# Two rows of layer 1's modulation move from the ctx attention to the heads of two feed forwards

## The chip, the cores and the metric

The kernel runs on one core of one Trainium2 chip. The metric is the device time of one execution in microseconds (us), the median of the runs.

## The reference

The program computes two blocks on 256 tokens of width 1024, all in float32. The first block has two layers; each is a feed forward, a mixer (convolution, recurrence, pool), a cross attention and a second feed forward, with a layer norm behind each. The second block also has two layers, on the output of the first and on a ctx stream of 256 tokens; each has an attention and a PEER feed forward, and both are modulated by six vectors per layer:

```python
def swiglu(x, w_gate, w_up, w_down):
    return (jax.nn.silu(x @ w_gate) * (x @ w_up)) @ w_down
...
for l in range(DEPTH):                       # first block
    h = layer_norm(ALPHA * h + 0.5 * swiglu(h, ffn1...), ...)
    ...mixer, layer_norm; cross_attn, layer_norm...
    h = layer_norm(ALPHA * h + 0.5 * swiglu(h, ffn2...), ...)
...
mod = silu(c) @ ada_w[i] + ada_b[i]          # second block, layer i: 6 x 1024 values, for c and for c_ctx
```

The modulation of layer 1 is what the change moves about: a product of two vectors of 1024 values (for the two conditions) with a 1024 x 6144 matrix.

## The kernel before, in words

**Two streams of work.** TensorE (PE) is led through one long sequence. First comes the ctx stream of the second block's layer 0: modulation, QKV, an attention over the ctx (functions `ctx_attention`), the output projection and the PEER scores. Then comes the first block with its four feed forwards, two per layer. Beside the feed forwards VectorE (DVE) does the PEER work of the ctx stream: GpSimd (POOL) gathers expert rows of 1024 values by indirect DMAs, and DVE dots and sums them. Last comes the second block.

**Weights in chunks.** Most weights pass through a ring `wring` of four slots, each a chunk of 128 x 1024 float32 (512 KB). SyncE (SP) issues the loads in a fixed order (`load`, `chunk_loads`, L495 to L510); each waits until the chunk before in its slot is released (`chunk_done`). Feed forward weights have places of their own in `ring` (`ff_loads`, L512 to L518), three parts per tile and two tiles deep, but their loads stand in the same queue of SP. What SP waits for holds back all that stands behind it in the order.

**Rows of the modulation.** Layer 1's modulation has 6144 columns, made in 12 rows of 512 columns. A row takes four chunks, one turn of the ring (`mod_row_loads`, L528). It is multiplied in one of two ways. PE does it alone (`mod_row_part`, L833 to L843): eight matmuls of 128x2 by 128x512, two records each in the trace. Or DVE does it (`mod_row_sums`, L3084 to L3098): eight instructions scale the row's parts by the condition and add them up in `row_acc`, and PE sums that over the partitions with one product (L1526, two records). The last of the eight instructions releases all four chunks at once. Either way ScalarE (ACT) copies the 2x512 result and stores it (`mod_row_take`, L1749 to L1766).

**Where the rows stood.** Rows 0 and 1 are multiplied by PE in the ctx attention (L1146 to L1161), row 2 in the PEER scores of the ctx (L1265). In each layer of the first block, one row is summed by DVE at the end of each of the two feed forwards, and one is multiplied by PE in the layer norm behind the cross attention and one in the norm behind the second feed forward. The last row comes at the second block's start.

**The ctx attention.** It has four units of heads. For each, PE computes scores (L1124), DVE takes the maximum and negates it (L2578, L2580), ACT takes the exponentials (four pieces), DVE divides by the sum (L2587, L2589), PE transposes the probabilities (L1133), ACT copies them, and PE multiplies them with the values (L1142). PE's order is written out by hand: scores 0, half of row 0, scores 1, the other half, transposes and values of unit 0, scores 2, row 1, unit 1, scores 3, unit 2, unit 3, then the output projection (L763). DVE puts tiles of the first layer's modulation (`ada_tiles`, L2362 to L2376, two instructions of 128x1024 each that matter here) between its softmax steps; the gated add of the projection is L2598.

**A feed forward.** It has 22 tiles: the first, five turns of a loop of four, and the last. For each tile PE makes gate and up (L1494, 32 records), ACT applies silu, DVE multiplies (`hidden_tile`, L3064), and PE adds the down product (L1502, 16 records) one tile later. DVE's sum of a row stands behind the loop, ahead of the last hidden tile; its column sum on PE stands between the last two down products. The row's chunks are loaded ahead of the loop, so that they lie ready. The loads of the next chunks (the norm's row, or the first mixer weights) stand behind the loop's in SP's queue and wait for the release by DVE's sum.

## Time and profile before

| | |
|---|---|
| median of 3 runs | 3305.03 us (3302.08 to 3306.79) |
| profiled execution, its own time | 3290.4 us |
| its span | 3288.5 us |
| PE busy | 3084.1 us (94%) |
| PE weight loads (PEld) | 2185.8 us (66%) |
| DVE busy | 2111.8 us (64%) |
| POOL busy | 1221.7 us (37%) |
| ACT busy | 951.1 us (29%) |
| DMA | 1165.52 MB, mean 354 GB/s |

The profiled execution is one run, and its time can be set against its span only; the median comes from other runs. Busy shares are means over stages with different limits. In a row of the timeline the first number is the start in us from the span's begin, the second the duration; "x8" stands for eight instructions drawn together, and the bracket tells how long the engine was idle before it and what ended that.

### The profile page before, as it was taken

The numbers are of one execution on the slowest core, as the hardware profiler recorded it, in microseconds if no ns is written. First come the engines' busy times: TensorE is split into PE (matmuls) and PEld (weight loads), VectorE is DVE, ScalarE is ACT, GpSimd is POOL, SyncE is SP. The second block draws the span as 40 slices with busy tenths as digits, with TensorE's granted clock in tenths as the row PEclk, the third lists the DMA queues.
The fourth block names the chain that finished last, engine by engine and source line by source line (L and its number), as shares of the span: only waits on it lengthen the run. The fifth ranks groups of instructions, "written<-read, shape, count | busy, mean of one in ns | idle before, by whom it ended". The sixth has DMA issues, their size and how long they took to land.

```text
span 3288.5 us, 39667 instructions
## 1 busy us (share of the span) xinstructions
PE 3084.1 (94%) x13217; PEld 2185.8 (66%) x13217; DVE 2111.8 (64%) x4281; ACT 951.1 (29%) x2489; POOL 1221.7 (37%) x1129
## 2 busy tenths in 40 slices
PE   8999999999999999999999999978989999997777
PEld 5598888887887888887886755533435855542224
DVE  6776787766555456765455596577565587587544
ACT  2310012121001002221002364335446464444333
POOL 1003554343444442353440144434444045454332
PEclk9999999999999999999999999999999999999999
DMA  9687988788998996788996799999999799999998
GB/s 351 215 299 287 374 339 305 267 325 338 356 347 336 365 345 231 242 326 338 370 355 241 292 421 420 420 419 404 410 422 420 293 419 421 421 421 422 421 421 356
DMA packets 252614, 1165.52 MB, mean 354 GB/s; under 512 B 27321, under 2 KB 34969, under 8 KB 186417
## 3 DMA queue, kind: packets, MB, share of 16 engines
q0 software_dynamic: 152784, 825.30, 62.3%
q1 hardware_dynamic: 99632, 338.30, 28.4%
q8 instruction: 80, 1.31, 0.2%
q14 instruction: 70, 0.57, 0.0%
q10 hardware_dynamic: 48, 0.05, 0.0%
HBM read 1162.44 MB, written 1.10 MB: 354 GB/s over the span
## 4 chain that ended last, share of the span: by engine, by line
PE 65%; DMA 17%; DVE 7%; ACT 5%; issue 2%; SPq 0%; POOL 0%; ACTq 0%; DVEq 0%; POOLq 0%
PE ps_b L1494 18%; PE ps_a L1432 13%; DMA ring<-in_peer_uv,idx 12%; PE ps_a L1502 9%; PE ps_b L776 6%; PE ps_a L763 5%; ACT arena L1721 3%; DVE ring L2883 2%; DMA arena<-in_peer_uv,idx 2%; DMA wring<-in_second_w 2%; PE ps_b L785 1%; PE ps_b L1261 1%; ACT L1721 1%; PE ps_b L1202 1%; PE ps_b L1254 1%
## 5 line engine op out<-in xcount | busy, mean ns | idle before, releaser
L1432 PE MATMUL ps_a<-ring,arena 128*128 128x512 f32 x1728 | 823.3, 611 | 131.0 <-ACT arena L1721 130.4
L738 POOL DMA_INDIRECT ring<-in_peer_uv,idx x448 | 498.4, 1112 | 888.7 <-PE ps_a L1432 624.7
L2883 DVE SCALAR_TENSOR_TENSOR ring<-ring,h_tm 128x1024 f32<-128x1024 f32 x448 | 546.6, 1222 | 381.7 <-DMA ring<-in_peer_uv,idx 381.0
L697 POOL DMA_INDIRECT ring<-in_peer_uv,idx_now x512 | 577.1, 1127 | 427.9 <-DVE arena L2711 163.8
L1432 PEld LDWEIGHTS ps_a<-ring,arena 128*128 128x128 f32 x1728 | 309.3, 192 | 564.5 <-ACT arena L1721 291.3
L1494 PE MATMUL ps_b<-x_t,ring 128*128 128x256 f32 x2816 | 623.6, 380 | 2.0 <-DMA ring<-in_ffn 1.1
L1494 PEld LDWEIGHTS ps_b<-x_t,ring 128*128 128x128 f32 x2816 | 533.0, 190 | 81.5 <-issue 3.5
L1721 ACT ACTIVATE arena<-ps_b 128x256 f32<-128x256 f32 (+3 forms) x226 | 103.6, 460 | 1254.7 <-PE ps_b L1494 829.5
L1502 PE MATMUL ps_a<-arena,ring 128*128 128x256 f32 x1408 | 318.7, 380 | 0.0
L2711 DVE SCALAR_TENSOR_TENSOR arena<-ring,h_tm 128x1024 f32<-128x1024 f32 x256 | 299.4, 1219 | 25.0 <-DMA ring<-in_peer_uv,idx_now 24.5
L1502 PEld LDWEIGHTS ps_a<-arena,ring 128*128 128x128 f32 x1408 | 267.5, 190 | 39.3 <-issue 3.5
L1721 ACT ACTIVATE wts<-dots 128x1 f32<-128x1 f32 (+1 forms) x514 | 103.7, 202 | 606.3 <-DVE ring L2883 523.6
L3064 DVE SCALAR_TENSOR_TENSOR arena<-ps_b,arena 128x256 f32<-128x256 f32 x88 | 37.3, 424 | 336.3 <-PE ps_b L1494 193.1
L1721 ACT ACTIVATE arena<-consts,wts 128x128 f32<-128x128 f32 x512 | 205.5, 401 | 66.5 <-PE ps_a L1432 20.7
L776 PE MATMUL ps_b<-x_t,wring 128*128 128x256 f32 x896 | 197.8, 381 | 6.6 <-ACT x_t L1721 6.6
L2720 DVE SCALAR_TENSOR_TENSOR arena<-ring,stage,arena 128x1024 f32<-128x1024 f32 x160 | 195.1, 1277 | 4.0 <-DMA ring<-in_peer_uv,idx_now 3.9
L776 PEld LDWEIGHTS ps_b<-x_t,wring 128*128 128x128 f32 x896 | 166.9, 190 | 34.0 <-issue 8.1
L763 PE MATMUL ps_a<-arena,wring 128*128 128x256 f32 (+1 forms) x896 | 169.1, 350 | 1.9 <-DMA wring<-in_second_w 1.0
L763 PEld LDWEIGHTS ps_a<-arena,wring 128*128 128x128 f32 x896 | 150.6, 191 | 20.1 <-issue 2.0
L1721 ACT ACTIVATE wts<-wts,gates 128x1 f32<-128x1 f32 x512 | 150.7, 294 | 16.6
L2720 DVE SCALAR_TENSOR_TENSOR arena<-ring,wts,arena 128x1024 f32<-128x1024 f32 x92 | 115.0, 1287 | 49.5 <-DMA ring<-in_peer_uv,idx_now 49.5
L1721 ACT ACT_TABLE_LOAD x107 | 137.3, 1283 | 12.0 <-PE ps_b L1494 8.7
(444 smaller groups left out, 3341.0 us busy)
## 6 DMA issues: line engine op xcount, KB each, us to landing
ring<-in_ffn SPq DMA_DIRECT2D x264, 512.0 KB, 7.1
wring<-in_second_w SPq DMA_DIRECT2D x174, 512.0 KB, 5.3
wring<-in_mix_w SPq DMA_DIRECT2D x128, 512.0 KB, 5.7
ring<-in_ada_rows POOLq DMA_DIRECT2D x36, 512.0 KB, 6.3
ring<-in_second_w SPq DMA_DIRECT2D x12, 1024.0 KB, 9.9
ring<-in_peer_uv,idx_now POOLq DMA_INDIRECT x512, 8.6
ring<-in_peer_uv,idx POOLq DMA_INDIRECT x448, 14.8
arena<-in_second_w SPq DMA_DIRECT2D x13, 512.0 KB, 8.1
```

What stands on the lines that cost most here:

```text
L697: G.indirect_dma_start(rows[:, s, :], None, table, bass.IndirectOffsetOnAxis(ap=idx_now[:, half, s:s + 1], axis=0)).then_inc(rows_in[s], p ...
L738: G.indirect_dma_start(pairs[slot].rearrange("p c d -> p (c d)"), None, a["peer_uv"], bass.IndirectOffsetOnAxis(ap=idx[:, b, s:s + 1], axi ...
L763: ins = mm(acc_t[:, j, cols], w[:, k * P:(k + 1) * P], src[:, k, cols], start=k == 0, stop=k == KT - 1)
L776: ins = mm(bank[:, t * T:(t + 1) * T], w[:, k * P:(k + 1) * P], src[:, k, :], start=k == 0, stop=k == KT - 1)
L1432: ins = mm(ps_a[:, b * D + j * 512:b * D + (j + 1) * 512], diags[:, at % DIAGS, :], pairs[at % PAIRS][:, 1, j * 512:(j + 1) * 512], start= ...
L1494: ins = mm(bank[:, part * T:(part + 1) * T], fw[:, ft % 2, part, k * P:(k + 1) * P], x_t[:, k, :], start=k == 0, stop=k == KT - 1)
L1502: ins = mm(acc_t[:, j, :], fw[:, ft % 2, 2, j * P:(j + 1) * P], hidden[:, ft % 2, :], start=False, stop=last, skip_group_check=True)
L1721: return nc.scalar.activation(out, in_, func, **k)
L2711: V.scalar_tensor_tensor(acc[s % 2], rows[:, s, :], 1.0, h, ALU.mult, ALU.mult, accum_out=out).then_inc(row_used, ve.adds(row_used))
L2720: ins = V.scalar_tensor_tensor(acc[s % 2], rows[:, s, :], w, acc[s % 2], ALU.mult, ALU.add)
L2883: V.scalar_tensor_tensor(row, row, 1.0, h_tm[:, n // SLOTS, :], ALU.mult, ALU.mult, accum_out=dots[:, n % SLOTS:n % SLOTS + 1]).then_inc(d ...
L3064: V.scalar_tensor_tensor(hidden[:, ft % 2, :], ps_b[:, (ft % 2) * 512 + T:(ft % 2 + 1) * 512], 0.5, silu[:, ft % 2, :], ALU.mult, ALU.mult ...
```

## The change

- **ctx attention.** Rows 0 and 1 are no longer multiplied there; the only row of the ctx stage (row 0) is the one in the PEER scores. The output projection's weights (WO) are loaded right behind QKV's, ahead of row 0. DVE's order becomes: three times "weights of unit u, maximum of unit u+1, one modulation tile", then the weights of unit 3 and two tiles. Before, one tile stood behind unit 3.
- **Head of two feed forwards.** Row 3 is summed by DVE ahead of the first hidden tile of layer 0's second feed forward, row 6 at the same place of layer 1's first. Their chunks are loaded where the end's row was loaded before, ahead of the loop. PE's column sum for them (`row_total`) stands behind the loop, ahead of the last tile's gate and up; ACT takes it ahead of the last silu.
- **End of the same two.** Their end rows (4 and 7) remain, but their loads now stand behind the loop's loads in SP's queue. DVE's sum of any row but the first waits until PE has summed the row before (`row_summed`), as both use `row_acc`.
- The other rows keep their places with new numbers: `FF_ROWS` at the ends, `NORM_ROWS` in the norms, and `ROW_AT` maps row numbers to columns.

```diff
--- before
+++ after
@@ -54,8 +54,9 @@
 MOD_ROWS = ADA_CHUNKS // WR
-CTX_MOD_ROWS = 3
-ROW_AT = 0, 1, 2, 4, 3, 5, 6, 7, 8, 9, 10, 11
+CTX_MOD_ROWS = 1
+ROW_AT = 0, 4, 1, 5, 6, 2, 7, 8, 3, 9, 10, 11
+FF_ROWS, HEAD_ROWS, NORM_ROWS = ((1, 4), (7, 9)), (3, 6), ((2, 5), (8, 10))
@@ -71,6 +72,9 @@
 ROW_LOADS = (FIRST_ADA - WR + QKV_CHUNKS + WO_CHUNKS + 2 * PQ_CHUNKS) // WR + CTX_MOD_ROWS + 1
+MIX_LOADS = MIX_CHUNKS // WR
+ROW_TURNS = {row: ROW_LOADS + turns for row, turns in (
+    (1, 0), (3, MIX_LOADS + 2), (4, MIX_LOADS + 3), (6, MIX_LOADS + 5), (7, MIX_LOADS + 6), (9, 2 * MIX_LOADS + 8))}
@@ -532,10 +536,8 @@
             eng.dma_start(subk, a["subk"]).then_inc(subk_in, 16)
+            chunk_loads(a["second_w"], FIRST_ADA + QKV_CHUNKS, WO_CHUNKS)
             mod_row_loads(0)
-            mod_row_loads(1)
-            chunk_loads(a["second_w"], FIRST_ADA + QKV_CHUNKS, WO_CHUNKS)
-            mod_row_loads(2)
             chunk_loads(a["second_w"], FIRST_ADA + PQ_AT, PQ_CHUNKS)
@@ -546,25 +548,28 @@
             for l in range(L):
-                mix_at, row_at = l * MIX_CHUNKS, CTX_MOD_ROWS + 4 * l
+                mix_at = l * MIX_CHUNKS
                 for w in range(2):
...
                             ff_loads(l * (2 * FT) + (w * FT + ft), ft, part)
-                    if w == 0:
-                        mod_row_loads(row_at)
+                    if w == 1:
+                        chunk_loads(a["mix_w"], mix_at + (MIX_CHUNKS - WR), WR)
+                        mod_row_loads(NORM_ROWS[l][0])
+                    if w != l:
+                        mod_row_loads(HEAD_ROWS[l])
                     else:
-                        chunk_loads(a["mix_w"], mix_at + (MIX_CHUNKS - WR), WR)
-                        mod_row_loads(row_at + 1)
-                        mod_row_loads(row_at + 2)
+                        mod_row_loads(FF_ROWS[l][w])
                     with sp.loop(FT_TURNS, **ff_turn) as i:
...
                                 ff_loads(i * FT_STEP + (l * (2 * FT) + (w * FT + 2 + ft)), ft, part)
+                    if w != l:
+                        mod_row_loads(FF_ROWS[l][w])
                     if w == 0:
...
                     else:
-                        mod_row_loads(row_at + 3)
+                        mod_row_loads(NORM_ROWS[l][1])
             def place_load(place, chunk_at, landed):
@@ -1133,9 +1138,7 @@
                     ins.then_inc(pt_done, pe.adds(pt_done))
-                if u < 2:
-                    mod_row_free()
-                else:
+                if u >= 2:
                     eng.wait_ge(pv_taken, pe.next(pv_taken))
@@ -1147,12 +1150,9 @@
                 qk_stats(4, 3, False)
-                mod_row_part(0, 0, 2)
                 ctx_scores(1)
-                mod_row_part(0, 2, WR)
                 ctx_weighted(0)
                 ctx_scores(2)
-                mod_row_part(1, 0, WR)
                 ctx_weighted(1)
@@ -1481,7 +1481,17 @@
-            def feed_forward(h_ready):
+            def row_total():
+                pe.skip(chunk_done, WR)
+                for arrived in weights_in:
+                    pe.skip(arrived, 16)
+                eng.wait_ge(chunk_done, pe.now(chunk_done))
+                mod_row_free()
+                mm(ps_d[0:2, :], mean_d[:, 0:2], row_acc, start=True, stop=True).then_inc(
+                    row_summed, pe.adds(row_summed))
+                pe.skip(mod_row_taken, 1)
+
+            def feed_forward(h_ready, two_rows):
@@ -1517,15 +1527,11 @@
                         down(q)
+                if two_rows:
+                    row_total()
                 gate_up(FT - 1)
                 down(FT - 2)
-                pe.skip(chunk_done, WR)
-                for arrived in weights_in:
-                    pe.skip(arrived, 16)
-                eng.wait_ge(chunk_done, pe.now(chunk_done))
-                mm(ps_d[0:2, :], mean_d[:, 0:2], row_acc, start=True, stop=True).then_inc(
-                    row_summed, pe.adds(row_summed))
-                pe.skip(mod_row_taken, 1)
+                row_total()
                 down(FT - 1, True)
@@ -1582,7 +1588,7 @@
             for l in range(L):
-                feed_forward(h_take if l else h_have)
+                feed_forward(h_take if l else h_have, l == 1)
                 layer_norm(value_between)
@@ -1691,7 +1697,7 @@
                 layer_norm(mod_row_between, True)
-                feed_forward(h_take)
+                feed_forward(h_take, l == 0)
                 layer_norm(mod_row_between, l + 1 < L)
@@ -1942,12 +1948,10 @@
                 exps(0)
-                mod_row_take(0, 0, ada_row[0])
                 turned(0)
...
                 exps(2)
-                mod_row_take(1, 1, ada_row[1])
                 turned(1)
@@ -2006,7 +2010,7 @@
                 act(lbs[:, 8:16], lbs[:, 0:8], ACT.Exp).then_inc(lb_exp, ac.adds(lb_exp))
-                mod_row_take(2, 1, ada_row[0])
+                mod_row_take(0, 1, ada_row[0])
                 for b in range(NB):
@@ -2191,7 +2195,7 @@
-            def feed_forward():
+            def feed_forward(head_row=None):
                 def tile(ft):
@@ -2203,6 +2207,8 @@
                         ac.skip(hidden_done, 1)
+                if head_row is not None:
+                    mod_row_take(head_row, 2, mod_row)
                 eng.wait_ge(hidden_done, ac.now(hidden_done))
@@ -2223,10 +2229,9 @@
             for l in range(L):
-                row_at = CTX_MOD_ROWS + 4 * l
                 eng.wait_ge(layer_vecs, ac.next(layer_vecs))
-                feed_forward()
-                mod_row_take(row_at, 2, mod_row)
+                feed_forward(HEAD_ROWS[1] if l == 1 else None)
+                mod_row_take(FF_ROWS[l][0], 2, mod_row)
                 layer_norm(0)
@@ -2253,7 +2258,7 @@
                     if g == 8:
-                        eng.wait_ge(mod_row_out[row_at % 2], ac.now(mod_row_out[row_at % 2]))
+                        eng.wait_ge(mod_row_out[FF_ROWS[l][0] % 2], ac.now(mod_row_out[FF_ROWS[l][0] % 2]))
                     group(g, dst)
@@ -2309,11 +2314,11 @@
                 layer_norm(2)
-                mod_row_take(row_at + 1, 1, mod_row)
-                feed_forward()
-                mod_row_take(row_at + 2, 2, mod_row)
+                mod_row_take(NORM_ROWS[l][0], 1, mod_row)
+                feed_forward(HEAD_ROWS[0] if l == 0 else None)
+                mod_row_take(FF_ROWS[l][1], 2, mod_row)
                 layer_norm(3)
-                mod_row_take(row_at + 3, 1, mod_row)
+                mod_row_take(NORM_ROWS[l][1], 1, mod_row)
@@ -3026,16 +3031,12 @@
             qk_norm(3, False, 0)
-            ve.skip(chunk_done, 2 * WR)
-            ctx_over(0)
-            ctx_max(1)
-            ada_tiles(1)
-            ctx_over(1)
-            for u in range(2, 4):
-                ctx_max(u)
-                ada_tiles(4 - u)
+            for u in range(3):
                 ctx_over(u)
-            ada_tiles(1)
+                ctx_max(u + 1)
+                ada_tiles(1)
+            ctx_over(3)
+            ada_tiles(2)
             ve.skip(pt_done, 8)
@@ -3081,13 +3082,14 @@
-            def mod_row_sums(l, w):
-
-                loads = ROW_LOADS + l * (MIX_CHUNKS // WR + 4) + w * (MIX_CHUNKS // WR + 2)
+            def mod_row_sums(row):
+
+                if row > CTX_MOD_ROWS:
+                    eng.wait_ge(row_summed, ve.next(row_summed))
                 for k in range(KT):
...
                     if k % 2 == 0:
-                        eng.wait_ge(weights_in[k // 2], 16 * loads)
+                        eng.wait_ge(weights_in[k // 2], 16 * ROW_TURNS[row])
                     if k == 0:
@@ -3119,13 +3121,12 @@
                     if q == FT - 2:
-                        mod_row_sums(0, 0)
+                        mod_row_sums(FF_ROWS[0][0])
                 eng.wait_ge(row_used, ve.now(row_used))
...
                 eng.wait_ge(dve_step, ve.now(dve_step))
-                for i, out_done in enumerate(mod_row_out):
-                    eng.wait_ge(out_done, 16 * ((CTX_MOD_ROWS + 1 - i) // 2))
+                eng.wait_ge(mod_row_out[0], 16 * CTX_MOD_ROWS)
                 V.memset(attn, 0.0).then_inc(dve_step, ve.adds(dve_step))
@@ -3134,6 +3135,8 @@
+                if w != l:
+                    mod_row_sums(HEAD_ROWS[l])
                 hidden_tile(0)
@@ -3143,7 +3146,7 @@
                     turn_end(summing, i, at + HEAD_SLOTS)
-                mod_row_sums(l, w)
+                mod_row_sums(FF_ROWS[l][w])
                 hidden_tile(FT - 1)
```

## Rows read from the trace of the kernel before

**Rows 1.** The page's chain of work that ended last, share of the span by engine
```profile
PE 65%; DMA 17%; DVE 7%; ACT 5%; issue 2%; SPq 0%; POOL 0%; ACTq 0%; DVEq 0%; POOLq 0%
```

**Rows 2.** Busy us: PE, PEld, DVE, ACT, POOL; PE clock, DMA share, GB/s
```profile
86.00:127.00 41.00, 34.26 (x117) 15.19 (x116) 30.99 (x44) 18.60 (x50) 2.65 (x5) 1.00 0.52 175
...
775.00:975.00 200.00, 199.61 (x924) 175.25 (x923) 105.78 (x106) 7.51 (x20) 93.12 (x92) 1.00 0.97 365
```

**Rows 3.** Timeline, ctx attention: start, us, engine, line, operation, out<-in, idle before <-releaser
```profile
88.82 3.60 PE L839 MATMUL ps_b<-wring,cond 128*2 128x512 f32 x8
...
93.91 1.22 DVE L2589 TENSOR_TENSOR arena<-arena,stats 128x1024 f32<-128x1024 f32 x1
...
100.31 1.96 PE L1142 MATMUL ps_b<-arena,vals 128*128 128x512 f32 x4 [1.42 <-ACT arena L1721]
...
102.10 1.89 PE L1124 MATMUL ps_a<-keys_t,arena 128*128 128x256 f32 x8
...
103.92 7.03 PE L839 MATMUL ps_b<-wring,cond 128*2 128x512 f32 x16
...
105.49 0.47 ACT L1721 ACTIVATE arena<-ps_a,stats 128x256 f32<-128x256 f32 x1 [2.59 <-DVE stats L2580]
...
106.85 0.48 ACT L1721 ACTIVATE arena<-ps_a,stats 128x256 f32<-128x256 f32 x1
...
111.88 0.60 ACT L1721 ACTIVATE arena<-ps_c 128x512 f32<-128x512 f32 x1 [0.31 <-ACT arena L1721]
...
114.90 1.89 PE L1124 MATMUL ps_a<-keys_t,arena 128*128 128x256 f32 x8
...
122.25 0.66 PE L1133 MATMUL ps_c<-consts,arena 128*128 128x128 f32 x4 [1.80 <-DVE arena L2589]
...
124.17 1.95 PE L1142 MATMUL ps_b<-arena,vals 128*128 128x512 f32 x4 [0.83 <-ACT arena L1721]
...
126.86 27.87 PE L763 MATMUL ps_a<-arena,wring 128*128 128x256 f32 x128 [0.73 <-issue]
...
134.15 0.88 DVE L2598 SCALAR_TENSOR_TENSOR ctx_t<-ps_a,mods,ctx_t 128x256 f32<-128x256 f32 x2 [4.15 <-PE ps_a L763]
```

**Rows 4.** Timeline, two pauses of PE, and busy times just behind the second
```profile
39.02 9.32 PE L776 MATMUL ps_b<-arena,wring 128*128 128x256 f32 x32 [3.10 <-ACT arena L1721]
...
2940.50 2.99 PE L1432 MATMUL ps_a<-ring,arena 128*128 128x512 f32 x4 [2.90 <-ACT arena L1721]
...
2942.00:2943.00 1.00, 1.00 (x2) 0.34 (x1) 1.00 (x9) 0.73 (x3) 0.00 (x0) 0.50 1.04 434
```

**Rows 5.** Timeline, DVE's first hidden tile of layer 0's second feed forward
```profile
768.41 0.42 DVE L3064 SCALAR_TENSOR_TENSOR arena<-ps_b,arena 128x256 f32<-128x256 f32 x1 [6.99 <-PE ps_b L1494]
```

**Rows 6.** Timeline, end of layer 0's second feed forward
```profile
965.84 10.69 SPq L515 DMA_DIRECT2D ring<-in_ffn  x4
...
975.87 7.07 PE L1494 MATMUL ps_b<-x_t,ring 128*128 128x256 f32 x32
...
978.76 5.75 DVE L3095 SCALAR_TENSOR_TENSOR arena<-wring,cond,arena 128x512 f32<-128x512 f32 x7
...
984.53 2.16 SPq L498 DMA_DIRECT2D wring<-in_second_w  x4
...
986.32 1.02 PE L1526 MATMUL ps_d<-arena,consts 128*2 128x512 f32 x2
...
987.27 3.72 PE L1502 MATMUL ps_a<-arena,ring 128*128 128x256 f32 x16
...
990.92 1.45 PE L839 MATMUL ps_b<-wring,cond 128*2 128x512 f32 x3
```

**Rows 7.** DMA at that end: busy times, then issues from 984 and from 970 us
```profile
975.00:985.00 10.00, 10.00 (x48) 8.82 (x47) 9.48 (x13) 0.38 (x1) 3.91 (x4) 1.00 0.89 319
...
wring<-in_second_w SPq DMA_DIRECT2D x3, 512.0 KB, 5.6
...
ring<-in_ffn SPq DMA_DIRECT2D x7, 512.0 KB, 10.3
```

## The prediction

> **What bounds the kernel now.** I read the chain of waits first: TensorE (PE) holds 65% of it, DMA 17%, VectorE (DVE) 7% [rows 1]. Then the busy times by stretch, because a share over the whole span hides that the two places touched have different limits. In the loop of a feed forward PE is busy for 199.6 of 200 us while DVE has 94 us free and the DMA engines are at 0.97 [rows 2]. In the ctx attention PE is busy for 34 of 41 us and the DMA engines are at 0.52 [rows 2]. Last I read the timeline of the ctx attention [rows 3]: 14 us of PE's time there is the product of two modulation rows. It stands between the steps of a softmax, in which PE, ScalarE (ACT) and DVE wait for each other in turn. So one must ask which of these PE microseconds anybody waits for. A PE microsecond in a feed forward, by contrast, is paid in full.
>
> **Sum, part 1: two rows leave the ctx attention.** Removed are 32 matmul records on PE (3.60, as much again later, and 7.03 us [rows 3]), two ACT copies, two stores and 4 MB of loads (eight chunks of 0.52). I rebuild the chain with the intervals of the trace that stay:
> - The weights of unit 0 are ready at 95.13 (93.91 + 1.22). The transposes now start there. From transposes to the value product it is 1.92 us (122.25 to 124.17), from there to the scores of unit 2 1.79 us (100.31 to 102.10), from these to unit 2's exponentials 3.39 us (102.10 to 105.49). That gives 102.3 instead of 105.49.
> - The exponentials take 1.84 us (105.49 to 106.85 + 0.48). ACT's own order puts the copies of unit 1's transposes behind them, so these come at 104.2 instead of 111.88; the 7.03 us of PE's row work had pushed them far beyond. From those copies to unit 3's scores it is 3.02 us (111.88 to 114.90), so 107.2 instead of 114.90.
> - From there to the output projection at 126.86 nothing changes. **The term is -7.7 us** [rows 3]. The other 6.5 us of removed PE work become pauses.
>
> DVE must not take PE's place. One tile of the first layer's modulation moves behind the last softmax step, ahead of the first gated add. DVE idles 4.15 us before that add [rows 3], a tile costs two instructions of 1.22 us as the other 128x1024 ones here: hidden. The loads of the output weights now directly follow QKV in SyncE's (SP's) queue: earlier, never later.
>
> **Part 2: the clock in the new pauses.** Without the row work two PE pauses of about 3.5 us appear: one where 3.6 us of it stood ahead of unit 0's transposes, one ahead of unit 1's value product (101.9 to 105.4 in the rebuilt chain). This trace has ten PE pauses of 2.4 us or more after the start, the first and the last of which are shown; near seven of them the granted clock went to 0.50, the 1.2 GHz level, and back to 1.00 some 3.3 us later [rows 4]. Work paced by PE in such a stretch takes twice the time: 1.65 us at most per pause. The longest such fall made 32 matmuls take 9.32 [rows 4] instead of 7.07 us [rows 6]: 2.25 us. Bounds for two pauses are 0 and 4.5. **I take +2.3 us**: seven in ten times twice 1.65.
>
> The Trainium skill ("TensorE: Matmul & The Clock Gate", section "HAM oscillation") speaks against this change: idle gaps throttle the array again, so filler work is not free to remove. By that rule both pauses lose the clock, which makes this term 3.3 and the total 1.0 worse; the trace mostly agrees, with three of ten pauses that kept it.
>
> **Part 3: the sums at the head (rows 3 and 6).** Each is eight DVE instructions of 128x512, about 6.2 us (5.75 for seven of them [rows 6]). DVE idles 6.99 us there before the first hidden tile in layer 0 [rows 5], and in layer 1 about as long. The loads are issued where two loads ahead of the loop were issued before; the last chunk's slot is freed by PE when the norm row ends, which is about when tile 0's products start. Those take 7.07, like any tile's; a landing of 5.6 [rows 7] and the sum's last two instructions (1.6) fit in beside them. At worst the hidden tile is half a microsecond late in layer 1, and PE has tile 1's products, another 7 us, before it needs it. **0 us.** Were that cover gone, each late microsecond would cost one. The gathers behind it are caught up with DVE's free 47% [rows 2].
>
> **Part 4: the ends of those two feed forwards.** This is where the change pays. Call T the start of the last tile's gate and up products (975.87 in layer 0) [rows 6].
> - Each head row adds one column sum on PE: it costs 0.95 (986.32 to 987.27, where the last down product starts). **+1.9 us** for two, in full.
> - The row summed at the end (rows 4 and 7) used to be loaded ahead of the loop. Now its four loads wait in SP's queue behind the last feed forward load, which leaves SP at about T+0.7 (965.84 + 10.69 [rows 6]). Four take 2.16 us to issue [rows 6], so the last leaves at T+2.8. With the landing of the nearest small group, 5.6 [rows 7], it is there at T+8.4, and the sum, two instructions (1.6) later, at T+10.0: in time, as PE gets to the column sum at T+11.4 (10.45 + 0.95). But the stretch is not free: 319 GB/s flow there at a share of 0.89 [rows 7]. From about T+1, when the full rate ends, some 4.6 MB are asked for (four gathers, the last feed forward load, the row, at 0.52 MB each), which take 12.3 us at the loop's 365/0.97 = 376 GB/s [rows 2], 10.7 at the 434 of the stretch in [rows 4]. The row's last part then lands between T+11.7 and T+14.1, the sum comes 1.6 later, and PE waits 1.9 to 4.3. The bytes bind more than a landing measured beside one small load, so I take 2.8 from within that span; bounds 0 and 4.3 each. **+5.6 us** for two.
> - What is queued behind: all four slots are released by the last instruction of that sum. So the next loads (norm row 5, or the first mixer weights) leave SP only then; before, at 984.53, 2.7 us ahead of the down product. After the sum, PE has column sum and down product, 4.5 us (0.95 and 3.6, 987.3 to 990.92), until it wants the first of them. Landing takes 5.6 [rows 7]; at most 6.4 (984.53 to 990.92), as PE did not wait at 990.92. So PE waits between 1.1 and 1.9, and I take 1.2, near the landing measured, each: **+2.4 us** for two.
>
> The Trainium skill ("DMA: Bandwidth & Descriptors", "Queues, rings and completion order") says that a DMA engine serves its queues in turn, packet by packet. By that rule neither side can starve the other: with equal halves the row's last part lands together with the last gather, near the late bound, and the total would be up to 3 us worse. This trace shows mixed rates, not whose packet went first.
>
> **Total:** -7.7 + 2.3 + 1.9 + 5.6 + 2.4 = +4.5 us. The profiled execution took 3290.4 (span 3288.5, the rest lies around it), the median of the runs is 3305.03; the same difference on it gives **3309.5 us**. The ends of the bounds are -7.7 + 0 + 1.9 + 0 + 2.2 = -3.6 and -7.7 + 4.5 + 1.9 + 8.6 + 3.8 = +11.1. About 0.2% (6.6 us) is what a measurement of this kernel can tell from no change.
>
> **Rivals.**
> - **The row work set the pace in the ctx attention.** Then all 14.2 us come off, and with part 4's certain 1.9 alone it ends at 3292.7. For: PE is 34 of 41 us busy. Against: PE had waits of 1.42 and 1.80 there even with the row work, and ACT's order cannot be passed. Chance 0.04.
> - **The ends are covered.** Rows and next loads land in time and the clock holds: -7.7 + 1.9, 3299.2. For: a landing of 5.6. Against: 4.5 us of work against a landing of 5.6 or more, and the bytes asked for. 0.10.
> - **DVE takes PE's place** in the ctx attention, so that nothing comes off: part 4's 9.9 alone, 3314.9. Against: DVE idle before the add. 0.05.
> - **Late landings, the one that ends slower.** The place is the end of the two feed forwards: if both the row and the next loads take 10.3 to land, as feed forward loads did in the stretch around that end [rows 7], the sum ends at T+14.7, 3.3 behind PE, and the wait in the norm is 5.8 (10.3 - 4.5). With 0.95 that is 10.05 per end; -7.7 + 2.3 + 20.1 = +14.7, 3319.7. It decides from 6 us per end on. For: DMA at 0.97 in the loop. Against: that number is of loads queued behind 2 MB of others. 0.14.
>
> My forecast has 0.67. Faster by over 0.2% is the first rival: 0.04. Slower is the fourth (0.14), the third (0.05) and the upper end of the forecast's bounds, past +6.6, to which I give 0.11: 0.30. The rest, 0.66, is within 0.2%. The range takes in the forecast's bounds, the second and third rivals and, all but, the fourth: 3299 to 3319, leaving out the first and half of the fourth.
>
> **What would show it.** The output projection starts near 119.2, or 121.5 with the clock lost, and PE has two pauses of 3 us or more before it, with clock records of 0.50. DVE's sums stand ahead of the first hidden tile without a new wait on PE. At the two ends there are two column sums; DVE's sum sits at T+8 to T+14; a PE wait on the row sum and one on a load of second_w or mix_w appear. I am wrong if the projection starts later than 123, if a head sum ends after tile 1's products, or if the ends cost under 2 or over 8 us each.

## The result, and the profile after

Over eight runs of each kernel the changed kernel takes 3316.59 us (median, 3312.98 to 3322.58) against 3302.03 before (3299.55 to 3306.79): 14.6 us more, a ratio of 1.0045, 95% interval 1.0036 to 1.0054. It is slower by more than 0.2%.

The profiled execution of after has a span of 3312.1 us, 23.6 more than the first trace of before. That is 9 more than the medians differ, so the two spans can't be subtracted as a whole. A comparison by stages says more, with two further traces of before beside it. In the page the busy times and the chain hardly move:

```profile
span 3312.1 us, 39635 instructions
...
PE 3082.5 (93%) x13179; PEld 2189.6 (66%) x13189; DVE 2123.3 (64%) x4297; ACT 950.0 (29%) x2489; POOL 1223.5 (37%) x1129
...
PE 65%; DMA 17%; DVE 7%; ACT 5%; issue 2%; SPq 0%; POOL 0%; another core or an unknown queue 0%; DVEq 0%; ACTq 0%; POOLq 0%
```

PE has 1.6 us less to do, although some of it ran at half clock, and the kernel is slower: the loss is in PE's waits. The chain is that of [rows 1] to the per cent, and so tells nothing here. The busy times by stretch do (columns as in [rows 2]):

```profile
86.00:123.00 37.00, 24.20 (x82) 14.50 (x82) 28.10 (x39) 17.43 (x48) 2.11 (x4) 0.86 0.18 63
94.00:98.00 4.00, 2.45 (x9) 2.05 (x10) 3.93 (x6) 1.72 (x5) 0.00 (x0) 0.56 0.00 0
107.00:111.00 4.00, 3.47 (x5) 1.61 (x6) 1.40 (x2) 0.65 (x2) 0.53 (x1) 0.64 0.38 131
771.00:971.00 200.00, 199.53 (x924) 174.91 (x923) 105.48 (x106) 7.66 (x20) 93.85 (x92) 1.00 0.96 364
975.00:980.00 5.00, 5.00 (x25) 4.41 (x24) 0.00 (x0) 0.00 (x0) 1.71 (x2) 1.00 0.97 344
980.00:985.00 5.00, 4.11 (x20) 3.27 (x18) 1.45 (x3) 0.38 (x1) 0.00 (x0) 1.00 1.03 418
985.00:990.00 5.00, 0.00 (x0) 0.00 (x0) 3.74 (x6) 0.00 (x0) 0.00 (x0) 0.87 0.32 130
990.00:995.00 5.00, 4.38 (x8) 2.23 (x9) 2.42 (x4) 0.59 (x1) 0.00 (x0) 0.50 0.67 237
```

The ctx attention is shorter, but its mean clock is 0.86 where it was 1.00: the second and third lines are its two stretches of low clock. The loop of the feed forward is what it was. In the last four lines, the end of layer 0's second feed forward, PE stands still from 985 to 990 us, and then works at 0.50.

The timeline of the ctx attention, to set beside [rows 3]:

```profile
87.54 1.02 PE L869 MATMUL ps_a<-arena,consts 128*128 128x512 f32 x2
...
94.87 1.12 PE L1138 MATMUL ps_c<-consts,arena 128*128 128x128 f32 x4 [3.47 <-DVE arena L2594]
...
97.52 3.78 PE L1145 MATMUL ps_b<-arena,vals 128*128 128x512 f32 x4 [0.69 <-ACT arena L1727]
...
101.10 1.98 PE L1129 MATMUL ps_a<-keys_t,arena 128*128 128x256 f32 x8
...
107.53 3.26 PE L1145 MATMUL ps_b<-arena,vals 128*128 128x512 f32 x4 [3.58 <-ACT arena L1727]
...
130.30 0.88 DVE L2603 SCALAR_TENSOR_TENSOR ctx_t<-ps_a,mods,ctx_t 128x256 f32<-128x256 f32 x2 [1.55 <-PE ps_a L768]
```

The two forecast pauses are there, 3.47 and 3.58 us, and behind each the value product takes nearly twice its 1.96 us. The output projection starts at 123.01, against 126.86. DVE still idles before the gated add, 1.55 us, so it did not take PE's place.

The end of layer 0's second feed forward, beside [rows 6]:

```profile
972.53 1.02 PE L1490 MATMUL ps_d<-arena,consts 128*2 128x512 f32 x2
972.77 0.33 SPq L519 DMA_DIRECT2D ring<-in_ffn  x1
973.31 19.03 SPq L502 DMA_DIRECT2D wring<-in_second_w  x8
...
982.31 0.48 DVE L3094 TENSOR_SCALAR arena<-wring,cond 128x512 f32<-128x512 f32 x1 [7.43 <-DMA wring<-in_second_w]
...
984.79 1.54 DVE L3097 SCALAR_TENSOR_TENSOR arena<-wring,cond,arena 128x512 f32<-128x512 f32 x2 [1.21 <-DMA wring<-in_second_w]
987.31 3.25 DVE L3097 SCALAR_TENSOR_TENSOR arena<-wring,cond,arena 128x512 f32<-128x512 f32 x4 [0.98 <-DMA wring<-in_second_w]
...
990.62 1.87 PE L1490 MATMUL ps_d<-arena,consts 128*2 128x512 f32 x2 [6.50 <-DVE arena L3097]
...
992.41 5.26 PE L1512 MATMUL ps_a<-arena,ring 128*128 128x256 f32 x16
...
997.60 1.88 PE L844 MATMUL ps_b<-wring,cond 128*2 128x512 f32 x4
```

The row's chunks are asked for from 973.3 on. DVE waits three times for one; PE then waits 6.50 us for DVE. The column sum and the last down product behind the wait take 1.87 and 5.26 us instead of 1.02 and 3.72, and the norm's row (997.60) finds its chunks there. The other end is the same picture with a wait of 7.07.

**Where the time went.** The table has stages cut at PE's timeline, in us: to the start of the output projection; from there to the first feed forward; then feed forwards two and three (first gate product to the first product of the norm behind); and the two mixers with their cross attentions (norm to the next feed forward). "Again" and the pair are traces taken for the experiments below.

| trace | to projection | scores | mixer 0 | ff two | ff three | mixer 1 |
|---|---|---|---|---|---|---|
| before | 126.86 | 109.77 | 293.84 | 230.52 | 230.42 | 286.97 |
| before, again | 126.07 | 109.65 | 291.79 | 231.20 | 230.69 | 287.36 |
| before, pair | 126.58 | 113.18 | 294.12 | 230.52 | 230.21 | 286.88 |
| after | 123.01 | 107.81 | 296.12 | 240.73 | 240.08 | 292.98 |
| after, pair | 121.54 | 108.76 | 290.83 | 238.51 | 239.37 | 286.88 |

Before the first feed forward the change gains 5.8 us (3.85 and 1.96) between the first two traces. The two feed forwards lose 10.2 and 9.7. That is +14.1, and the medians say +14.6. That the two agree so well is in part luck: the sum leaves out the mixers, which differ by 2.3 and 6.0 us between these two traces, and the gain of 5.8 came out smaller when it was measured alone (`ctx_alone`).

### The profile page after: what moved, and what is told of

Read it like the earlier page. It is cut to its first block, busy times and chain, and to the rows that moved or that the text cites. A ratio compares the mean times of both kernels' runs of the same rounds, so it can differ in the third digit from the quotient of the medians.

```text
span 3312.1 us, 39635 instructions
## 1 busy us (share of the span) xinstructions
PE 3082.5 (93%) x13179; PEld 2189.6 (66%) x13189; DVE 2123.3 (64%) x4297; ACT 950.0 (29%) x2489; POOL 1223.5 (37%) x1129
## 4 chain that ended last, share of the span: by engine, by line
PE 65%; DMA 17%; DVE 7%; ACT 5%; issue 2%; SPq 0%; POOL 0%; another core or an unknown queue 0%; DVEq 0%; ACTq 0%; POOLq 0%
PE ps_b L1504 17%; PE ps_a L1432 13%; DMA ring<-in_peer_uv,idx 11%; PE ps_a L1512 9%; PE ps_b L781 5%; PE ps_a L768 5%; DMA arena<-in_peer_uv,idx 3%; ACT arena L1727 3%; DMA wring<-in_second_w 2%; DVE ring L2888 2%; PE ps_b L1261 2%; PE ps_b L790 1%; PE ps_b L1254 1%; PE ps_b L1202 1%; ACT L1727 1%
## 5 line engine op out<-in xcount | busy, mean ns | idle before, releaser
L2716 DVE SCALAR_TENSOR_TENSOR arena<-ring,h_tm 128x1024 f32<-128x1024 f32 x256 | 299.3, 1221 | 20.5 <-DMA ring<-in_peer_uv,idx_now 14.6
```

What stands on the lines that cost most here:

```text
L2716: V.scalar_tensor_tensor(acc[s % 2], rows[:, s, :], 1.0, h, ALU.mult, ALU.mult, accum_out=out).then_inc(row_used, ve.adds(row_used))
```

## The experiments

Where a ratio is given, it is to the kernel before in runs on the same chip. Its median was 3287.9 us beside the first set, 3303.05 beside the second and 3288.37 beside the third, so absolute times are comparable within a set alone.

**First set: is the account additive, and is it only these places?**

`before_again` is the unchanged kernel.

> The unchanged kernel before, for a second trace. Theory A (the change acts at three places only: ctx attention with the scores behind it, and the two feed forward ends): between the end of layer 1's first feed forward and the start of the second block this trace takes about as long as the changed kernel's, some 6 us longer than the first trace of before did, and the span is near 3298 to 3303. Theory B (the change also costs something further back, in layer 1's mixer): this trace repeats the first one there within 1 us and the 6.3 us stay a difference of the kernels.

It took 3289.66 us with a span of 3287.7. Its layer 1 mixer is 287.36 us, that of the first trace within 0.4. By its own expectation this spoke for theory B, a cost in the mixer; but the runs of before beside this trace have a median 14 us below that of the runs beside after's, so the chip was another. The pair of the third set decides it.

`ctx_alone`:

```diff
-(1, 0), (3, MIX_LOADS + 2), (4, MIX_LOADS + 3), (6, ...
+(1, 0), (4, MIX_LOADS + 2), (7, MIX_LOADS + 4), (9, 2 * MIX_LOADS + 6)
...
-                    if w != l:
-                        mod_row_loads(HEAD_ROWS[l])
-                    else:
-                        mod_row_loads(FF_ROWS[l][w])
+                    mod_row_loads(FF_ROWS[l][w])
...
-                if w != l:
-                    mod_row_sums(HEAD_ROWS[l])
```

> The changed kernel without the two head rows (rows 3 and 6 of the modulation are not computed, the results of rows 4 and 7 are stored in their places); the end rows are loaded ahead of the loop again. Theory A: the ctx part alone gains what the traces show at the first feed forward's start, 5.8 us: 0.9982 of before, about 3296. Theory B (the gain of the ctx part is given back later, because the stage behind waits for something else): 1.000, within 1 us of before.

Measured: 3284.55 us, 0.9989 (0.9980 to 0.9998), which is 3.6 us less than before by the ratio and 3.35 by the medians. That lies between the two theories, and theory A's 0.9982 is still inside the interval. The projection starts at 123.31, the first feed forward at 232.34, 3.4 us earlier than in `before_again`, and nothing of it is given back: both feed forwards have 231.12 and 229.50 us. The ctx part gains, but some 3.5 us rather than 5.8. Its projection starts as in after; what is smaller is the gain in the scores stage (109.03 us here, 107.81 in after, 109.65 to 113.18 in the traces of before). The next run, which has the old ctx attention, takes 108.67 there, so that this stage differs from trace to trace by as much as the gain in it.

`heads_alone`: after, with rows 0 and 1 put back on PE, fourteen rows in all.

```diff
-CTX_MOD_ROWS = 1
-ROW_AT = 0, 4, 1, 5, 6, 2, 7, 8, 3, 9, 10, 11
+CTX_MOD_ROWS = 3
+ROW_AT = 5, 7, 0, 4, 1, 5, 6, 2, 7, 8, 3, 9, 10, 11
...
+                mod_row_part(0, 0, 2)
                 ctx_scores(1)
+                mod_row_part(0, 2, WR)
                 ctx_weighted(0)
                 ctx_scores(2)
+                mod_row_part(1, 0, WR)
```

> The changed kernel with two rows multiplied by PE in the ctx attention again, in the old order (fourteen rows, two of them double). Theory A: each of the two ends costs 9.9 us (0.95 column sum, 6.5 to 7.1 wait for the row's sum, 2.4 clock), so +19.8 over before: 1.0060, about 3322. Theory B (the ends' cost is largely slack that something later takes back): under +12.

Measured: 1.0058 (1.0046 to 1.0070), +19.1 us on 3287.9 (by the medians, 3308.88 us and +21.0). The feed forwards take 240.77 and 240.07 us, +9.6 and +9.4 against `before_again`. The answer for the column sum's source line over the whole trace, with what its engine waited for (us, times; matmul and weight load are counted each):

```profile
L1497 PE MATMUL ps_d<-arena,consts x12: 591/592/1061, 461.1 to 1764.2; 128*2 128x512 f32 x12
its engine sat idle before it (us, times) until:
  DVE arena L3110: 26.7, 4
```

That is two waits for DVE's sum, each counted for the matmul and for the weight load: some 6.7 us each. The cost of the ends is real, is there without the ctx part, and nothing takes it back. -3.6 of one and +19.1 of the other make +15.5 (+17.6 by the medians); the whole change measured +14.6. The parts add up within what the intervals leave open.

`spread_loads`:

```diff
-                    with sp.loop(FT_TURNS, **ff_turn) as i:
+                    turns = FT_TURNS - (w != l)
+                    with sp.loop(turns, **ff_turn) as i:
 ...
                     if w != l:
-                        mod_row_loads(FF_ROWS[l][w])
+                        for ft in range(FT_STEP):
+                            for part in range(3):
+                                ff_loads(turns * FT_STEP + (l * (2 * FT) + (w * FT + 2 + ft)), ft, part)
+                            load(ft, a["second_w"][LAYER_1 + WR * ROW_AT[FF_ROWS[l][w]] + ft])
```

> The changed kernel, but the end row's four chunks are loaded one behind each tile of the loop's last turn, not all four behind the loop. Theory A (the wait is the late, bunched loads): both waits of PE and both falls of the clock behind them vanish, two column sums of 0.95 stay; -5.8 + 1.9 = -3.9 against before, 0.9988, about 3298; 18 us under the changed kernel. Rival (DMA bandwidth is the limit and only moved): feed forward loads land later and PE waits inside the last turn, so that at most 6 of the 18 us come back.

Measured: 1.0009 (1.0000 to 1.0018), +3.0 us where -3.9 was expected and after has +14.6. The last tile of layer 0's second feed forward:

```profile
956.60 7.17 PE L1508 MATMUL ps_b<-x_t,ring 128*128 128x256 f32 x32 [1.00 <-DMA ring<-in_ffn]
963.61 3.62 PE L1516 MATMUL ps_a<-arena,ring 128*128 128x256 f32 x16
967.15 1.02 PE L1494 MATMUL ps_d<-arena,consts 128*2 128x512 f32 x2
968.11 7.17 PE L1508 MATMUL ps_b<-x_t,ring 128*128 128x256 f32 x32
975.12 3.62 PE L1516 MATMUL ps_a<-arena,ring 128*128 128x256 f32 x16
978.66 1.02 PE L1494 MATMUL ps_d<-arena,consts 128*2 128x512 f32 x2
979.61 3.72 PE L1516 MATMUL ps_a<-arena,ring 128*128 128x256 f32 x16
```

Between the last two down products PE waits for nobody, and the clock holds: moving the four loads alone removes both the wait and its clock term. The other end is the same. What stays is the column sum and a wait for a feed forward load in the last turn, 1.00 us here and 0.88 there, where before and after have none. The feed forwards take 233.22 and 232.66 us, +2.0 each, twice the 0.95 of the column sum. So the main theory holds for the end, and the rival is right in its direction but not its size: the loop has little DMA time to spare, and the added 2 MB cost PE about 1 us per feed forward there. By the traces the parts make -3.6 + 4.0, about nothing; the measured +3.0 has an interval from 0 to +5.9 us that takes this in.

**Second set: the clock, and what binds at the end.**

`fill_ctx`:

```diff
+            def ctx_filler(bank, n):
+                for _ in range(n):
+                    mm(ps_b[0:2, bank * 512:bank * 512 + T], cond[:, 0:2], keys_t[:, 0, 0:T], start=True, stop=True)
...
                 ctx_scores(1)
+                ctx_filler(0, 7)
                 ctx_weighted(0)
...
+                if u == 1:
+                    ctx_filler(1, 7)
                 if u >= 2:
                     eng.wait_ge(pv_taken, pe.next(pv_taken))
```

> The changed kernel with seven small products (cond by 256 columns of the keys, already in SBUF, results unused) put on PE ahead of unit 0's transposes and seven ahead of unit 1's value product, 3.3 us each, in the two new pauses. Theory A (the lost half of the ctx gain is the clock, which falls in those pauses): granted clock 1.00 throughout, the two value products take 1.96 us each instead of 3.78 and 3.26, and the output projection starts near 119.0 instead of 123.0: 3.9 us less than the changed kernel, 1.0033 of before. Theory B (the chain through ACT and DVE is longer than rebuilt): the projection starts no earlier than 121.5. Either way the stage behind may take back up to 2 us by its weights landing no earlier.

Measured: 1.0029 (1.0018 to 1.0040), 5.3 us less than after by the ratios (1.0045 - 1.0029 on 3303), with intervals that overlap, so that the time alone doesn't show the gain. The trace does. The busy times and the granted clock, over the two filled pauses and over a later stretch:

```profile
91.00:107.00 16.00, 14.43 (x65) 7.51 (x64) 14.64 (x20) 8.59 (x30) 1.06 (x2) 1.00 0.14 44
116.00:120.00 4.00, 3.39 (x4) 1.17 (x4) 3.73 (x8) 0.46 (x1) 0.53 (x1) 0.57 0.45 151
```

Over both filled pauses the clock stays at 1.00. In this execution it fell once later, near unit 3, where neither before nor after lost it: the value product there took 3.48 us. The projection starts at 120.83, of which 1.5 is that fall. `spread_fill`, below, has the same filler without it:

```profile
86.00:118.00 32.00, 25.44 (x108) 13.99 (x106) 27.46 (x39) 16.78 (x48) 2.12 (x4) 1.00 0.23 71
```

```profile
118.07 2.18 PE L772 MATMUL ps_a<-arena,wring 128*128 128x256 f32 x9 [0.73 <-issue]
```

Counted from the product ahead of the softmax (86.97 here, 87.54 in after, 87.87 in before), the projection comes 31.10 us later here, 35.47 in after and 38.99 in before. So the chain without the rows is 7.9 us shorter, and the two falls of the clock cost 4.4 of them.

`fill_ends`:

```diff
                 down(FT - 2)
+                if two_rows:
+                    for i in range(14):
+                        mm(ps_c[:, 0:T], mean_d, x_t[:, i % KT, :], start=True, stop=True)
                 row_total()
```

> The changed kernel with fourteen products of 128x256 (6.2 us, results unused) on PE in the two waits for the end row's sum. Theory A (of the 9.9 us per end, 2.4 are the clock that falls in the wait: column sum 1.87 instead of 1.02 us, last down product 5.26 instead of 3.72): the wait itself stays, the clock stays at 1.00, and each end is 2.4 shorter: 4.7 us less than the changed kernel, 1.0031 of before. Theory B (the slow products are slow for another reason, such as a busy SBUF or PSUM): nothing changes, 1.0045.

Measured: 1.0036 (1.0023 to 1.0049). The busy times over the filled wait, and over the column sum and down product behind it:

```profile
993.00:1000.00 7.00, 7.00 (x33) 5.57 (x31) 5.22 (x7) 0.00 (x0) 0.00 (x0) 1.00 0.42 159
1000.00:1003.00 3.00, 3.00 (x14) 2.23 (x13) 1.17 (x2) 0.59 (x1) 0.00 (x0) 1.00 0.99 386
```

The clock holds, the column sum takes 1.02 us again, and the feed forwards take 238.37 and 238.20 us: 2.4 and 1.9 less than in after. PE's wait is filled, not shortened (in layer 0 the fillers even overran DVE's sum, which was done at 998.08, by 1.5 us). Theory A holds in the trace; in the time the difference, 3 us of an expected 4.7, is inside the intervals. The end in layer 1 shows one thing more:

```profile
1250.34 1.02 PE L1490 MATMUL ps_d<-arena,consts 128*2 128x512 f32 x2 [0.48 <-DVE arena L3100]
1250.46 2.13 SPq L502 DMA_DIRECT2D wring<-in_mix_w  x4
1251.29 3.72 PE L1512 MATMUL ps_a<-arena,ring 128*128 128x256 f32 x16
...
1254.85 1.89 PE L1567 MATMUL ps_b<-wring,mem_t 128*128 128x256 f32 x8
```

The mixer's first chunks leave SP at 1250.46, as late as forecast, and the first product that needs them starts at 1254.85, straight behind the down product. So the first chunk landed within 4.4 us, and PE didn't wait for it although the clock held and only 4.5 us of work lay between.

`half_bytes`:

```diff
-                        mod_row_loads(FF_ROWS[l][w])
+                        for s in range(WR):
+                            eng.wait_ge(chunk_done, sp.next(chunk_done))
+                            eng.dma_start(wring[:, s, 0:512],
+                                          a["second_w"][LAYER_1 + WR * ROW_AT[FF_ROWS[l][w]] + s][:, 0:512]).then_inc(
+                                              weights_in[s], sp.adds(weights_in[s], 16))
...
-                    part, weight = wring[:, k // 2, k % 2 * 512:(k % 2 + 1) * 512], cond[:, 2 * k:2 * k + 1]
+                    half = 0 if row in (4, 7) else k % 2
+                    part, weight = wring[:, k // 2, half * 512:(half + 1) * 512], cond[:, 2 * k:2 * k + 1]
```

> The changed kernel, but the end rows of the two feed forwards load only half of each chunk (columns 0 to 511, which are then used twice, so that rows 4 and 7 of the modulation differ). Theory A (bytes asked for at the end bind): with 1.05 MB less the last part lands some 2.5 us and the sum ends 4 us earlier; PE waits about 2.5 instead of 6.5 to 7.1, and the clock may fall less: 8 to 11 us less than the changed kernel, 1.0012 to 1.0021 of before. Theory B (the four loads leave too late, and their latency binds, whatever their size): the wait stays above 5 us, 1.004.

Measured: 1.0030 (1.0020 to 1.0040).

```profile
991.37 1.44 PE L1494 MATMUL ps_d<-arena,consts 128*2 128x512 f32 x2 [4.23 <-DVE arena L3102]
```

The waits are 4.23 and 3.88 us, 2.3 and 3.2 shorter than in after; the feed forwards take 237.70 and 236.24. The clock still falls: the last down products take 4.94 and 5.27 us. Neither theory's number is met (the time is some 5 us below after's, where 8 to 11 or nothing was expected). 1.05 MB at the 418 GB/s of that stretch are 2.5 us, and that is about what came off: the bytes bind, but I had expected 4, counting DVE's work as covered as well. The remaining wait of some 4 us I put down to what shares the way, four gathers and a feed forward load, and to the loads' late start. That is argued: no run takes the gathers away from the end, or starts the loads earlier and leaves the rest alone.

`spread_fill` is `spread_loads` and `fill_ctx` together.

> Spread loads at the ends and the filler products in the ctx attention together. Theory A (both act on their own): what the filler gains over the changed kernel (3.9 us) comes off spread_loads too: 0.9997 of before, or 0.999 by the traces. Theory B (the filler's gain is taken back in the stage behind): no less than spread_loads, 1.0009.

Measured: 0.9994 (0.9985 to 1.0002), 3300.33 us against 3303.05. The projection starts at 118.07 and the first feed forward at 227.10, the earliest of all traces. The two feed forwards take 233.59 and 235.54: PE waits 1.67 and 2.12 us for a feed forward load of the last turn, and behind the second of these waits the granted clock is 0.50 from 1210.2 to 1213.5. Theory A fits, and theory B's 1.0009 is outside the interval, though `spread_loads` itself is only known to lie between 1.0000 and 1.0018. The kernel can't be told from before.

**Third set: the two mixers, and a wider spread.**

`before_pair`, `after_pair`: the two kernels on one chip.

> Before and after once more, on one chip, to see how much of the 23.6 us between the first two traces' spans is the pair of traces rather than the change. Theory A (three places only): on one chip the stages between the feed forwards' ends and the next feed forwards' starts (the two mixers, 286 to 301 us in the traces so far) agree within 2 us in the two kernels, and the spans differ by 14 to 16 us. Theory B (the changed kernel costs some 6 us more in layer 1's mixer): they differ there by 4 us or more on one chip too.

> The changed kernel on the same chip as before_pair, same expectations.

The two traces are in the table above. Layer 1's mixer takes 286.88 us in both; layer 0's is 3.3 us shorter in after, not longer. So neither theory is met as it was written: in layer 0 the kernels differ by more than 2 us, but the wrong way round for a cost. The 6 us of layer 1's mixer between the first two traces are therefore no cost of the change. All traces of the second set, on the chip with the longer time, have 291.8 to 293.6 there; those of the first and third, of either kernel, have 286.5 to 287.9. (Before itself was not traced on a chip of the slower kind.) The spans differ by 0.8 only, where 14 to 16 was expected. That execution of before was a long one, 3297.36 against a median of 3288.37, with 3.01 us of waiting for one load in the scores stage:

```profile
202.90 2.37 PE L1261 MATMUL ps_b<-arena,wring 128*128 128x128 f32 x13 [3.01 <-DMA wring<-in_second_w]
```

The two ends cost 8.0 and 9.2 us in the pair, with waits of 5.25 and 6.18:

```profile
983.33 1.85 PE L1490 MATMUL ps_d<-arena,consts 128*2 128x512 f32 x2 [5.25 <-DVE arena L3097]
1234.68 1.86 PE L1490 MATMUL ps_d<-arena,consts 128*2 128x512 f32 x2 [6.18 <-DVE arena L3097]
```

`wide_fill` is `spread_fill` with the chunks behind every second tile of the last two turns:

```diff
-                    turns = FT_TURNS - (w != l)
+                    turns = FT_TURNS - 2 * (w != l)
...
-                        for ft in range(FT_STEP):
+                        for ft in range(2 * FT_STEP):
...
-                            load(ft, ...)
+                            if ft % 2:
+                                load(ft // 2, ...)
```

> As spread_fill, but the end row's four chunks go one behind every second tile of the last two turns. Theory A (each extra chunk in the queue delays the feed forward loads behind it by its own 1.3 us, and a gap of two tiles lets them catch up): the waits of 1.0 to 2.1 us for a feed forward load in the last turn vanish, each end costs 1 to 1.5 us instead of 2 to 5: 0.9985 of before. Theory B (the queue is as full all through the loop): the waits stay, 0.9994.

Measured: 1.0001 (0.9992 to 1.0010). The waits only move:

```profile
916.15 3.38 PE L1516 MATMUL ps_b<-x_t,ring 128*128 128x256 f32 x10 [2.00 <-DMA ring<-in_ffn]
...
1164.03 2.21 PE L1516 MATMUL ps_b<-x_t,ring 128*128 128x256 f32 x9 [1.51 <-DMA ring<-in_ffn]
...
1206.43 2.86 PE L1516 MATMUL ps_b<-x_t,ring 128*128 128x256 f32 x12 [0.69 <-DMA ring<-in_ffn]
```

The feed forwards take 235.64 and 234.31. Behind the wait of 2.00 us the clock is 0.50 from 917.5 to 920.8, so that it costs more than its length. Theory B holds. At both places in the loop that were tried, some feed forward load behind the row's loads comes late, and two tiles between them don't make up for it. No version that computes all twelve rows beats the kernel before by more than its measurement can tell.

## Why the prediction was right in its range and wrong in its middle

The time lies inside the stated range of 3299 to 3319, but the change cost 10 us more than the 4.5 forecast, and it fell in a class that had 0.30. That it lies in the range is partly luck. The +14.6 is beyond the forecast's own upper bound of +11.1; the range reached further only because it took in most of the late-landing rival. And the range stood on 3305.03 for before, which measured 3302.03 beside after: on the old base the same difference ends at 3319.6. Two of the prediction's own signs of being wrong came true as well: the ends cost 10.2 and 9.7 us each, where over 8 was named (8.0 and 9.2 in the pair), and the projection started at 123.01, where later than 123 was named (121.54 in the pair).

- **The ctx chain, -7.7: right.** With the clock held it is 7.9 (`spread_fill`). The step that ACT's own order puts unit 1's copies behind the exponentials, and that half of the removed PE work turns into pauses, is what the trace shows.
- **The clock in the pauses, +2.3: too small.** It cost 4.4, near the upper bound of 4.5. The failed step is "seven in ten times twice 1.65", in both factors. First the chance: the clock fell at both pauses in after, `ctx_alone`, `spread_loads`, `half_bytes` and `fill_ends`, and at the first alone in `after_pair`, where that one fall lasted over the value product and the scores behind it (3.78 and 3.20 us) and cost nearly as much (35.00 us to the projection, against 31.10). In the old trace three of ten pauses kept it, and what set them apart stays open: one of them was 3.59 us long. Second the price: with both falls certain the term would have been 3.3, still 1.1 short. The 1.65 assumed that the clock is back some 3.3 us later, but it stayed low for much longer behind the first pause, here in after and in its pair (busy times, then the clock at 0.50):

```profile
94.50:101.20 6.70, 5.65 (x13) 3.18 (x14) 5.40 (x9) 3.02 (x10) 0.53 (x1) 0.50 0.14 47
92.60:102.70 10.10, 8.14 (x19) 5.14 (x20) 6.30 (x9) 3.62 (x11) 0.53 (x1) 0.50 0.17 52
```

The old trace had this too: the product of [rows 4] that lost 2.25 us stands in a stretch at 0.50 from 36.7 to 43.3. The Trainium skill ("TensorE: Matmul & The Clock Gate", section "HAM oscillation") says that idle gaps throttle the array again; behind eleven of the twelve pauses of these six traces that is what happened. Its consequence, that filler work isn't free to remove, is what `fill_ctx` shows: 6.4 us of useless products gave time back.
- **Not forecast: the scores stage.** After the projection another 2.0 us came off between the first two traces, 0.6 in `ctx_alone` against `before_again`. PE waits there for weights, 2.2 us in the first trace of before, 1.5 in the second and 3.9 in the pair's, 0.5 and 1.2 in those of after. The eight chunks that left SP's queue may be the cause, but `ctx_alone`, without them too, waits 1.7, and `heads_alone`, which has them, 1.1. The cause stays open, and so does whether the change has a part in it.
- **The head sums, 0: right.** In layer 0 the sum runs from 757.81 to 764.09 and the hidden tile comes at 764.89. In layer 1 the hidden tile is 0.4 us later than before, as allowed for. PE waits in neither:

```profile
757.81 0.48 DVE L3094 TENSOR_SCALAR arena<-wring,cond 128x512 f32<-128x512 f32 x1
758.33 5.76 DVE L3097 SCALAR_TENSOR_TENSOR arena<-wring,cond,arena 128x512 f32<-128x512 f32 x7
764.89 0.42 DVE L3065 SCALAR_TENSOR_TENSOR arena<-ps_b,arena 128x256 f32<-128x256 f32 x1 [0.80 <-ACT arena L1727]
```

- **The column sums, 0.95 each: right.**
- **The wait for the end row, 2.8 each: the term that failed most.** It was 6.50 and 7.07, and 5.25 and 6.18 in the pair, above the upper bound of 4.3. (That bound has a slip: 12.3 us from T+1 on end at T+13.3 and not at T+14.1, which makes it 3.5.) Two steps of it were wrong. First, the last landing. I took 4.6 MB at 376 to 434 GB/s from T+1 on. What moved in layer 0 of after between 973.0 and 988.4, when the traffic ended, was 5.02 MB at a mean of 326 GB/s: 316 up to 979, 411 up to 986 and 104 for the rest. (T is 972.5 there, the end of the loop, where the head row's column sum now starts.) The third chunk was awaited until T+14.8 and the last bytes came at T+15.9, where I had the row complete at T+14.1 at the latest. Second, DVE's work behind it: the last stall was for the third chunk, so four instructions, 3.25 us, stood behind it and not two (in layer 0 of the pair it was the fourth, with two). The chunks came 2.5 us apart, 210 GB/s, as the gathers went on beside them: between 979 and 984.8 SP's queue moved 1.22 MB and that of the gathers 1.17. The Trainium skill's rule ("DMA: Bandwidth & Descriptors", section "Queues, rings and completion order") that an engine serves its queues in turn fits this even share. By it I had put the total up to 3 us worse; that would have been nearer, but still 7 us short.
- **The clock behind that wait: left out.** Column sum and down product took 2.4 us longer per end. I had priced pauses in the ctx attention and forgotten that a wait of PE at the end is a pause as well. `fill_ends` shows it.
- **The next loads, 1.2 each: 0.** They left as late as forecast. In after PE's work behind the wait took 7.0 us at the low clock rather than 4.5, which covers them; but they would have been covered anyway. In `fill_ends` the work took 4.5 us and the first chunk was there within 4.4, where I had taken 5.6, the median of three other loads.

Per end that makes 0.95 + 6.8 + 2.4 = 10.1 where I had 0.95 + 2.8 + 1.2 = 4.95. The rival of late landings had the right place and sign. That its +14.7 is also the total is luck: its split of 3.3 for the row and 5.8 for the norm was not what happened, and its landing of 10.3 was too short, as the third chunk left SP at 974.17 and was awaited until 987.31, 13.1 us later.

## What to carry to other kernels

When work is moved, move its bytes on paper as well: here 4 MB left a stretch with the DMA engines at 0.52 for one at 0.97, and whether they stood at the end, in the last turn or over two turns, something waited. Read a pause of PE as its length plus the clock behind it; where products that nobody needs fill a pause for free, they can be worth their place: here the traces show it, the total times don't resolve it. And where loads from two queues overlap, reckon with the even share that was seen here, and count the consumer's whole work behind its last stall.

## What I had not expected of the hardware

- Removing 14 us of PE work from a chain that mostly waits for others cost 4.4 us of clock. Fourteen small products of 6.4 us in all, which nobody reads, brought them back (31.10 against 35.47 us).
- How long the clock stays low behind a pause. Behind pauses of nearly one length, 3.47 to 3.59 us, it was low for some 10 us, for 7, for 3 or not at all, in two executions of one kernel (`after_pair` and after). The price of a pause is not one number.
- The burst at the end was slow at its start and at its end: 316 GB/s up to 979, 411 up to 986, then 152 for the next 1 us, with the third chunk still awaited. A mean of 326 is what the sum should have used.
- The same stages differ by up to 6 us (layer 1's mixer, 286.9 and 293.0) between chips on which the kernel before has medians of 3288 and 3303 us. A pair of traces from one chip has to be had before a difference of that size is put down to a change.
